# Delta rule: the block inverse built in halves of 64 rows, with paired 64x64 products

## The reference, cut to what matters

```
def gated_delta_rule(q, k, v, g, beta):
    ...
    L = jnp.where(strict, jnp.einsum('bhncd,bhnsd->bhncs', kb, k) * decay, 0.0)
    eye = jnp.eye(CHUNK, dtype=q.dtype)
    T = lax.linalg.triangular_solve(eye + L, jnp.broadcast_to(eye, L.shape),
                                    left_side=True, lower=True, unit_diagonal=True)
    u = T @ vb
    w = T @ (kb * jnp.exp(g)[..., None])
    ...
    def step(state, inp):
        q_n, k_n, u_n, w_n, a_n, gl_n = inp
        v_new = u_n - jnp.einsum('bhcd,bhde->bhce', w_n, state)
        ...
```

## Time and profile before

| | us |
|---|---|
| median of 3 runs | 3027.58 |
| lowest, highest | 3024.53, 3027.93 |
| profiled execution | 3023.76 |
| its span in the trace | 3021.8 |
| delta rule's eight turns, about | 2008 to 2606 in the trace |
| a mid turn | 77.0 |

### The profile page before, as it was taken

The page is one execution under the profiler, slowest core; times in us unless marked ns, Lnnn a source line. Parts: engine busy times, 40 slices in busy tenths (PEclk is TensorE's granted clock), DMA queues, the critical chain, the costliest instruction groups (busy, mean ns, idle before and its releaser), DMA issues.

```text
span 3021.8 us, 40078 instructions
## 1 busy us (share of the span) xinstructions
PE 2872.6 (95%) x13693; PEld 2347.7 (78%) x13693; DVE 1678.1 (56%) x2532; ACT 1257.0 (42%) x1846; POOL 616.0 (20%) x593
## 2 busy tenths in 40 slices
PE   7999999999998999999889999979999999789998
PEld 6888877788887888886677888768888888667766
DVE  4444345554434664348646643466666666577773
ACT  4443242443323332224533322345544544456664
POOL 2000003100002530015325300132222222112221
PEclk9999999999999999999899999989999999899999
DMA  4333331233333553332026533221222221122211
GB/s 124 97 97 97 91 91 49 77 104 97 94 98 107 169 150 94 97 85 72 13 86 176 156 95 96 54 77 57 61 60 63 64 61 49 35 63 56 56 56 56
DMA packets 485297, 255.55 MB, mean 85 GB/s; under 512 B 18819, under 2 KB 479398, under 8 KB 485174
## 3 DMA queue, kind: packets, MB, share of 16 engines
q1 hardware_dynamic: 483856, 253.25, 29.5%
q10 hardware_dynamic: 1318, 0.69, 0.1%
HBM read 251.77 MB, written 2.13 MB: 84 GB/s over the span
## 4 chain that ended last, share of the span: by engine, by line
PE 73%; DVE 11%; issue 5%; ACT 5%; POOL 4%; DMA 0%; ACTq 0%; DVEq 0%; POOLq 0%; SPq 0%
PE bank L254 56%; PE bank L1702 4%; DVE gdn_blocks L2155 2%; POOL sumsq L584 1%; PE bank L2548 1%; ACT w_hi L236 1%; POOL ada_sum L584 1%; PE bank L1727 1%; PE bank L1728 1%; PE bank L1729 1%; DVE dsa_work L1455 1%; DVE prod L680 1%; DVE small L1453 1%; DVE w_lo L242 1%; DVE ada_hi L570 1%
## 5 line engine op out<-in xcount | busy, mean ns | idle before, releaser
L254 PE MATMUL bank<-x_hi,w_hi 128*128 128x512 f32 x2328 | 961.3, 413 | 8.7 <-issue 3.1
L254 PE MATMUL bank<-x_hi,w_lo 128*128 128x512 f32 x2328 | 917.5, 394 | 0.0
L254 PE MATMUL bank<-x_lo,w_hi 128*128 128x512 f32 x2328 | 916.9, 394 | 0.0
L242 DVE TENSOR_TENSOR w_lo<-w_raw,w_hi 128x1024 fp32r<-128x1024 f32 x430 | 547.4, 1274 | 639.9 <-ACT w_hi L236 633.3
L236 ACT ACTIVATE w_hi<-w_raw 128x1024 fp32r<-128x1024 f32 x430 | 451.3, 1053 | 452.2 <-PE bank L254 420.1
L254 PEld LDWEIGHTS bank<-x_hi,w_hi 128*128 128x128 f32 x2328 | 443.9, 191 | 117.2 <-issue 21.6
L254 PEld LDWEIGHTS bank<-x_hi,w_lo 128*128 128x128 f32 x2328 | 442.5, 190 | 96.0
L254 PEld LDWEIGHTS bank<-x_lo,w_hi 128*128 128x128 f32 x2328 | 444.3, 191 | 93.6 <-issue 9.4
L399 POOL TENSOR_TENSOR sumsq<-sumsq,sq 128x512 f32<-128x512 f32 x54 | 91.7, 1698 | 1357.2 <-ACT sq L385 1355.9
L254 PE MATMUL bank<-h_hi,w_hi 128*128 128x512 f32 x832 | 323.9, 389 | 4.0 <-DVE h_lo L2654 2.4
L254 PE MATMUL bank<-h_hi,w_lo 128*128 128x512 f32 x832 | 323.7, 389 | 0.0
(11 more groups left out here) (441 smaller groups left out, 3733.6 us busy)
## 6 DMA issues: line engine op xcount, KB each, us to landing
w_raw<-in_ffn_wi_dram SPq DMA_DIRECT2D x176, 512.0 KB, 3.8
w_raw<-in_ffn_wo_dram SPq DMA_DIRECT2D x64, 512.0 KB, 3.9
w_raw<-in_ada_w_dram SPq DMA_DIRECT2D x48, 512.0 KB, 4.9
w_raw<-in_a_w_in_dram SPq DMA_DIRECT2D x48, 512.0 KB, 3.9
w_raw<-in_b_w_in_dram SPq DMA_DIRECT2D x32, 512.0 KB, 4.1
w_raw<-in_ffn_wo_dram SPq DMA_DIRECT2D x32, 384.0 KB, 3.3
w_raw<-in_even_w_in_dram SPq DMA_DIRECT2D x16, 512.0 KB, 4.0
w_raw<-in_a_w_out_dram SPq DMA_DIRECT2D x16, 512.0 KB, 3.7
```

The lines of the kernel that those rows point to most:

```text
L242: dve.tensor_tensor(w_lo[s][:], w_raw[raw_of(b) % RAW][:], w_hi[s][:].bitcast(F32), ALU.subtract).then_inc(w_lo_done, 1)
L254: mm = pe.matmul(out, lhs[:, w], rhs(kt), start=first and kk == 0 and m == 0, stop=last and kk == len(kts) - 1 and m == 2)
```

## The change

It builds T from halves of 64 rows. With the two halves' diagonal parts (a: rows 0 to 63, b: rows 64 to 127) and the quarter C between them, each half needs only (1 + F)(1 + F^2), as it has four blocks of 16; the quarter of T is two products (y and at) of the halves' inverses with C. All products are now 64x64 by 64x64 (`halves`), those of half a and half b issued in turn, for both heads and four chunks: f, g, f2, v, y, at with 16 products each and c with 8. The groups f, g, f2 and v use operands on partitions 0 to 63 with an output on the same partitions, and 64 to 127 likewise; in y both outputs lie on 64 to 127, and in at both on 0 to 63, in two banks. P and PT become one operation each for both heads (P is kept in a compact form of 64 columns per chunk). The copies are of 64 partitions by 512. Ahead of each group PE counts one semaphore up (`halves_begun`), on which nobody waits. T lies in a new tile of 128x128 per chunk whose lower left quarter POOL sets to zero once before the first turn.

`GDN_BESIDE` and `GDN_SPLITS` give the units and roundings new places, the sums of the next pair go to the other banks, and DVE and ACT get new orders:

```diff
+INV_PART = 64
...
+            T = tile("gdn_T", 43, 2)[:, :].rearrange("p (c x) -> p c x", x=P)
+            XT, X, F, m, V1, F2, V, CY = Pw[0], Pw[1], W2[0], W2[1], W3[1], W5[0], W5[1], W3[0]
...
-            "mid": {"kt": "q0", "kk": "q1", "vt": "q2", "sel": "q3", "inv": "k0 k1 k2 k3 v00 v01", "f": "v02", "f2": "v03", "v1": "v10", "f4": "v11",
-                    "v2": "v12", "sums": "v13", "tt": "O0", "vn0": "O1", "ds0": "O2", "ks1": "O3", "vn1": "O4", "ds1": "O5", "ks2": "O6", "vn2": "O7",
-                    "ds2": "z00", "ks3": "z01", "vn3": "z02 z03", "o3": "z10 z11 z12 z13"},
...
-                      "mid": {"start": "q", "vc": "k", "g1": "v0", "g2": "v1", "tt": "Oa", "vn3": "Ob", "end": "z0 z1"},
...
+            "mid": {"kt": "q0", "kk": "q1", "vt": "q2", "sel": "q3", "inv": "k0 k1 k2 k3 v00 v01 v02", "c": "v03", "f2": "v10", "v": "v11", "y": "v12",
+                    "at": "v13", "vn0": "O0", "ds0": "O1", "ks1": "O2", "vn1": "O3", "ds1": "O4", "ks2": "O5", "vn2": "O6", "ds2": "O7",
+                    "ks3": "z00", "vn3": "z01 z02", "o3": "z03 z10 z11 z12 z13"},
...
+                      "mid": {"start": "q", "vc": "k", "f": "v0", "f2": "v1", "at": "Oa", "vn3": "Ob", "end": "z0 z1"},
...
+            a, b = slice(0, P // 2), slice(P // 2, P)
+
+            def halves(step, *ops):
+
+                pe.sem_inc(G.halves_begun, 1)
+                for c in range(2 * TT):
+                    for out, lhs, rhs in ops:
+                        mm = pe.matmul(out[:, c * INV_PART:(c + 1) * INV_PART], lhs(c), rhs(c), start=True, stop=True)
+                mm.then_inc(*H.pe.done(step))
+
+            def half_of(x, r):
+                return lambda c: x[r, c * INV_PART:(c + 1) * INV_PART]
+
+            def of_E(r, cols):
+                return lambda c: G.E[c // TT][r, (c % TT) * P + cols.start:(c % TT) * P + cols.stop]
...
-                for h in range(2):
-                    dve(f"PT_{h}")
-                    four(first(h), G.W1[h], G.E[h], f"f_{h}")
-                for h in range(2):
-                    four(second(h), G.E[h], G.W1[h], f"g1_{h}")
-                beside("f")
-                for h in range(2):
-                    dve(f"f_{h}")
-                    act(f"g1_{h}")
-                    four(first(h), G.W4[h], G.W3[h], f"f2_{h}")
-                for h in range(2):
-                    dve(f"v0_{h}")
-                    four(second(h), G.W3[h], G.W4[h], f"g2_{h}")
+                dve("PT")
+                halves("f", (first(0)[a], half_of(G.X, a), of_E(a, a)), (first(1)[b], half_of(G.X, b), of_E(b, b)))
+                halves("g", (second(0)[a], of_E(a, a), half_of(G.X, a)), (second(1)[b], of_E(b, b), half_of(G.X, b)))
+                halves("c", (first(0)[b], half_of(G.X, a), of_E(a, b)))
+                beside("c")
+                act("fb")
+                dve("gb")
+                halves("f2", (first(0)[a], half_of(G.m, a), half_of(G.F, a)), (first(1)[b], half_of(G.m, b), half_of(G.F, b)))
                 beside("f2")
-                for h in range(2):
-                    dve(f"f2_{h}")
-                    four(first(h), G.W1[h], G.W5[h], f"v1_{h}")
-                beside("v1")
-                for h in range(2):
-                    act(f"g2_{h}")
-                    four(second(h), G.W2[h], G.W1[h], f"f4_{h}")
-                beside("f4")
-                for h in range(2):
-                    act(f"f4_{h}")
-                    dve(f"v1_{h}")
-                    four(first(h), G.W3[h], G.W5[h], f"v2_{h}")
-                beside("v2")
+                act("f2a")
+                dve("f2b")
+                halves("v", (second(0)[a], half_of(G.F2, a), half_of(G.V1, a)), (second(1)[b], half_of(G.F2, b), half_of(G.V1, b)))
+                beside("v")
+                dve("vb")
+                act("c")
+                halves("y", (first(0)[b], half_of(G.CY, a), half_of(G.V, a)), (first(1)[b], half_of(G.V, b), half_of(G.XT, b)))
+                beside("y")
+                act("bt")
+                halves("at", (first(0)[a], half_of(G.V, a), half_of(G.XT, a)), (first(1)[a], half_of(G.CY, b), lambda c: G.T[b, c, b]))
+                beside("at")
                 if at.kind != "last":
-                    for h in range(2):
-                        dve(f"v2_{h}")
                     sums_next(j + 1)
-                beside("sums")
-                for h in range(2):
-                    dve(f"v2_{h}")
-                    four(second(h), G.W5[h], G.Pw[h], f"tt_{h}")
-                beside("tt")
-                if at.kind != "last":
-                    pe.wait_ge(*N.act.after("ss_k", j + 1))
+                dve("at")
+                act("ct")
...
-                        else:
-                            act(f"tt_{h}")
-                        pe.matmul(first(h)[:, (t % 2) * P:(t % 2) * P + P], G.W4[h][:, x], G.W1[h][:, 3 * P:4 * P] if t else G.v_tok[h][:, x],
+                        pe.matmul(first(h)[:, (t % 2) * P:(t % 2) * P + P], G.T[:, h * TT + t, :], G.W1[h][:, 3 * P:4 * P] if t else G.v_tok[h][:, x],
...
-                copies("g1", G.W4, second)
+                a, b = slice(0, P // 2), slice(P // 2, P)
+                pe("f")
+                run("fa", G.F[a, :], first(0)[a], ACT.Copy)
+                run("fb", G.F[b, :], first(1)[b], ACT.Copy)
+                pe("c")
+                run("c", G.CY[a, :], first(0)[b], ACT.Copy)
+                splits("f")
                 if more:
                     silu(0, i, at, odd)
-                copies("g2", G.W2, second)
+                pe("f2")
+                run("f2a", G.F2[a, :], first(0)[a], ACT.Copy)
+                splits("f2")
                 if more:
                     silu(1, i, at, odd)
                 if p is not None:
                     high(p)
+                pe("y")
+                run("y", G.CY[b, :], first(0)[b], ACT.Copy)
+                run("bt", G.T[b, :, b], halves(first(1)[b]), ACT.Copy)
                 if more:
+                    if p is not None:
+                        act.wait_ge(*GdnOut.dve.after("lo_1", p))
+                    squares(j + 1, odd)
                     conv(2, j + 1, i, at, odd)
                 else:
                     for h in range(2):
                         gate(h, at.through(f"z{h}", i), at.bank(f"z{h}"), (tile_free, BANKS + at.tile[f"z{h}"]))
-                copies("f4", G.W3, second)
+                pe("at")
+                run("ct", G.T[a, :, b], halves(first(1)[a]), ACT.Copy)
                 if more:
-                    if p is not None:
-                        act.wait_ge(*GdnOut.dve.after("lo_1", p))
-                    squares(j + 1, odd)
                     sums(j + 1)
+                splits("at")
+                if more:
                     conv(3, j + 1, i, at, odd)
-                copies("tt", G.W4, second)
-                if more:
                     silu(2, i, at, odd)
...
-                full = [P, TT, P // INV_BLOCK, INV_BLOCK]
-                for h in range(2):
-                    tt(f"P_{h}", G.Pw[h][:, :].rearrange("p (t b i) -> p t b i", t=TT, i=INV_BLOCK), of_block(G.inv, h).to_broadcast(full),
-                       own_block[:, :].rearrange("p (t b i) -> p t b i", t=1, i=1).to_broadcast(full), ALU.mult)
-                for h in range(2):
-                    own(f"P_{h}")
-                    dve.transpose(G.W1[h][:], G.Pw[h][:]).then_inc(*done(f"PT_{h}"))
+                full, a, b = [P, 2 * TT, INV_PART // INV_BLOCK, INV_BLOCK], slice(0, P // 2), slice(P // 2, P)
+                tt("P", G.XT[:, :].rearrange("p (c b i) -> p c b i", c=2 * TT, i=INV_BLOCK), G.inv.rearrange("p c (b i) -> p c b i", b=1).to_broadcast(full),
+                   own_block[:, :].rearrange("p (c b i) -> p c b i", c=1, i=1).to_broadcast(full), ALU.mult)
+                own("P")
+                dve.transpose(G.X[:], G.XT[:]).then_inc(*done("PT"))
+
+                def halves(x):
+                    return x.rearrange("p (c x) -> p c x", x=INV_PART)
+
+                def eye(r):
+                    return ident[r, r].rearrange("p (c x) -> p c x", c=1).to_broadcast([P // 2, 2 * TT, INV_PART])
                 if more:
                     if p is not None:
                         dve.wait_ge(*gdn_gate(at, i, 1)[3])
                     conv(0, j + 1, i, at, odd)
-                for h in range(2):
-                    pe(f"f_{h}")
-                    dve.tensor_copy(G.W3[h][:], first(h)[:]).then_inc(*done(f"f_{h}"))
+                pe("g")
+                for n, r, src in (("ga", a, second(0)), ("gb", b, second(1))):
+                    dve.tensor_copy(G.m[r, :], src[r]).then_inc(*done(n))
+                for n, r, src in (("ha", a, second(0)), ("hb", b, second(1))):
+                    tt(n, halves(G.V1[r, :]), halves(src[r]), eye(r), ALU.add)
+                pe("f2")
+                dve.tensor_copy(G.F2[b, :], first(1)[b]).then_inc(*done("f2b"))
                 splits("vc")
```

(50 more changed lines are left out.)

46 lines of the change are left out of this document (22 added, 24 removed), and 8 rows, old and new, of the table GDN_BESIDE.

## The result

The changed kernel took **3047.13 us** (median of 4 runs, 3044.09 to 3047.93) against 3027.56 us of the kernel before (4 runs, 3024.53 to 3027.93): ratio 1.0065, 95% interval 1.0048 to 1.0082. It is slower by 19.6 us where +9 was forecast. The profiled execution took 3047.69 us, its span is 3045.9 us. PE's share fell from 95% to 93% while the span grew. From here on, lines are those of the changed kernel (1718 issues the 64x64 products, 1994 is ACT's copies, 2173 and 2236 to 2254 DVE's).

What follows compares the result with a forecast made beforehand. PE's list was taken to bound each turn; six middle turns at 1.3 + 1.2 us gave +15, first and last turn -6, so +9 us: 3036 against 3027.6, own range 3028 to 3048, overall range 3017 to 3056.

Steps and rivals of the forecast that it cites:

- What goes, what comes on PE: PE's list per turn: 14.4 us of passes and a 1.0 us wait go, 7.4 us come, so 8.0 us shorter.
- The chain to `at`: From the v products through DVE and ACT to bt: 9.3 us against 3.9 of PE work, so PE waits 5.4 us.
- the length of gating and rounding: Two DVE steps in the chain ahead of `at`, taken as 1.2 and 1.1 us.
- What is late next: PE's further waits in a middle turn: 1.4 us ahead of the sums, then 1.7, and 0.8 at the state copy.
- The clock: Half-speed stretch of some 3.5 us behind the wait in each middle turn, costing 1.7 us, taken as 1.2 net.
- The waits of "about 4.5 us" in the last turn: PE's waits in the last turn, without conv(1) or SiLU in the chain; that turn gains some 3.5 us.
- Faster small products: Rival, all groups of 64x64 products: passes faster than 0.031 us; at half the pace 3011 us; chance 0.2.
- The clock holds: Rival: the clock stays up or its loss falls wholly into waits; +2 us, 3029; chance 0.2.
- Pairs that share columns don't overlap: Rival: passes cost up to 0.062 us; y and at alone 3052 us, all six groups 3084; chance 0.1.
- The rule cited: Some 60 cycles of overhead per matmul on PE, an estimated floor of 0.025 us a pass, just under the measured 0.031.
- ACT's longest wait ... ahead of silu(1), about 7 us: Sign for the profile after: ACT waits longest on conv(1)'s bank, about 7 us.
- a turn should last 79 to 80: Sign for the profile after: turn length 79 to 80 us; under 77 the forecast is wrong.

Runs made afterwards that it cites:

- conv_early: Changed kernel with DVE's conv(1) put back where it stood before the change, between ha, hb and f2b: 3014.19 us, ratio 0.9957 to the kernel before.
- filled24: Changed kernel with 24 products of constants that nobody reads put ahead of `at`, where PE waits: 3051.50 us, ratio 1.0094 to the kernel before.
- cp_units_low: Changed kernel with the moves of conv_early and pool_late, one projection unit moved from ahead of f to ahead of v, DVE's low(p) ahead of `at`: 2988.41 us, ratio 0.9874.
- pool_late: Changed kernel with POOL's wide operations in middle turns waiting for DVE's copy of `at` instead of vb: 3037.13 us, ratio 1.0040 to the kernel before.
- yc_unpaired: Changed kernel with ACT's y and bt copies ahead of silu(1), conv(1) early on DVE, and pair partners issued apart: 3044.01 us, ratio 1.0069 to the kernel before.
- y_first: Changed kernel with ACT's copies of y and bt ahead of silu(1) and high: 3034.57 us, ratio 1.0026 to the kernel before.

## Why the prediction was right, and where it was off

The sign, the place and the mechanism were right: a shorter PE list, turned into a slower kernel by a wait ahead of `at` for ACT's copy behind silu(1). conv_early shows the cause, as undoing one place in DVE's list gives 33 us back. By its steps, for a middle turn:

- *What goes, what comes on PE.* "PE's list is then 8.0 us shorter", of which 1.0 was a wait: 7.0 of work. Busy PE time at full clock fell from 76.0 to 70.5 (conv_early 70.57, filled24 75.88 less 5.4), 5.5. **This term was 1.5 us too large.** Summed from start to start, the removed passes took 13.9 instead of 14.4 us (the first group of rows 4 was read as steady pace). The new ones took 7.1; the 7.4 of the forecast had 0.4 for the entries in it, and these stand in the product ahead of each small group, which takes 0.32 to 0.40 us to the next start instead of 0.23 (cp_units_low), in five groups 0.7 us where the one wait before had cost 0.2. That leaves some 0.8 us, for the most part in full-size products just ahead of and behind PE's waits; no run isolates it.
- *The chain to `at`.* "PE waits 5.4 us ahead of at": 7.1. **The step that failed is the length of gating and rounding**, taken from rows where POOL was not beside them: 1.29 and 1.22 instead of 2.37 and 2.30. The change's diff shows POOL's start moved to vb, ahead of these two, and I did not follow POOL's queue. pool_late measures it: 2.1 us of wait, 10 us of time. The 5.0 us that it leaves are near the forecast.
- *What is late next.* 1.4, 1.7 and 0.8 forecast; 1.1, 1.2 and 0.7 in filled24. The 1.1 are in the changed kernel covered by its slower clock.
- *The clock.* One half-speed stretch of 3.5 us behind the wait was forecast; 7 to 10 us came, in the turn shown 4.6 of the 10.2 inside the wait itself. The slower products cost 2.5 us instead of 1.7, and 1.1 to 1.4 of them fell where PE would have waited instead of 0.5. The net price, 1.1 to 1.4 us against 1.2 forecast, was right by luck: two errors cancel. The granted clock of that turn was 0.94 where 0.97 was forecast.
- *Together*: 1.5 (list) + 1.1 (waits at full clock, 10.4 instead of 9.3) - 0.1 make 2.5 of the 2.6 us by which a middle turn missed; six of them are 15 us. The first turn gained 1.5 less and the last 0.4 more than forecast, and the unchanged rest was 1.7 shorter in the profiled run. The waits of "about 4.5 us" in the last turn had no working: PE's waits there rose by 3.3 us (5.4 to 8.7), so that its size came near is luck in part.
- *The rivals.* Faster small products: no, 0.031. The clock holds: no. Pairs that share columns don't overlap: they do, y at 1.08 us like v; yc_unpaired shows what it would have been, 0.75 us a group.
- *The rule cited* (the Trainium skill, TensorEngine Tiling (Array Packing), Instruction Overhead) put the floor of a pass at an estimate of 0.025 us. Lone 64x64 passes took 0.053 to 0.057, paired ones 0.031 each, so the floor does not decide here. The same page's Key Properties say that different tiles work in parallel; yc_unpaired agrees.

"ACT's longest wait ... ahead of silu(1), about 7 us" was 9.84; "a turn should last 79 to 80" was 82, outside it.

## What to carry to other kernels

When the list of the engine that bounds a kernel is shortened, what that gains is set by the orders of the engines that serve it: here the same shorter list gave +19.6 or -38 us, by four moves, three in those orders and one of a projection unit in PE's own list. For each copy that the bounding engine waits for, write down what stands ahead of it on its engine and what those wait for; then do the same for the next wait (y_first failed on that). And when a queue is moved, look up which operations it will run beside: durations read elsewhere may not hold beside other neighbours (1.29 us became 2.37).
